# Rotary embeddings: the rotated half made by VectorE across partitions, in place of a matmul with a constant matrix

## The reference

```python
def apply_rope(x, ang):
    d2 = x.shape[-1] // 2
    x1, x2 = xf[..., :d2], xf[..., d2:]
    c, s = cos(ang), sin(ang)
    return concatenate([x1 * c - x2 * s, x2 * c + x1 * s], axis=-1)
# retention: over all 128 features of a head, angles from the token's position
# axial: over the first 64 features with the row of the token, over the last 64 with its column,
#        so the partners lie 32 features apart
```

## Time and profile before

| | us |
|---|---|
| median of 3 runs | 1290.53 (1287.97 to 1294.03) |
| the profiled execution | 1291.3 |
| its span, first to last instruction | 1289.5 |
| TensorE busy | 1266.9 (98%) |
| VectorE busy | 870.5 (68%) |
| ScalarE busy | 718.4 (56%) |
| mean granted TensorE clock | 0.985 of full |

### The profile page before, as it was taken

How to read it: one execution, slowest core, us unless ns; L and a number is a source line. 1 busy time by engine, 2 the same in 40 slices (tenths; PEclk the granted TensorE clock), 3 DMA queues, 4 the chain that set the end, 5 groups by cost and what they waited for, 6 DMA issues and landing times.

```text
span 1289.5 us, 22440 instructions
## 1 busy us (share of the span) xinstructions
PE 1266.9 (98%) x8876; PEld 1171.4 (91%) x8876; DVE 870.5 (68%) x1140; ACT 718.4 (56%) x1070; POOL 49.8 (4%) x76
## 2 busy tenths in 40 slices
PE   8999999999999999999999999999999999999999
PEld 7998899999898779999999899889999988899998
DVE  6889878886889657555566676575555577655554
ACT  3676554444644557444457764665555667655554
POOL 0101000000111000000001000000000000000000
PEclk8899899999899999999999999999999999999999
DMA  9986889995699733555555544356565543466540
GB/s 352 376 305 239 300 269 333 330 332 202 218 346 354 240 83 130 197 197 197 201 187 191 173 148 154 131 179 208 200 195 196 196 146 99 137 206 204 199 163 34
DMA packets 147362, 275.54 MB, mean 214 GB/s; under 512 B 4728, under 2 KB 85392, under 8 KB 147161
## 3 DMA queue, kind: packets, MB, share of 16 engines
q1 hardware_dynamic: 132176, 220.21, 50.1%
q0 software_dynamic: 13872, 52.05, 11.8%
q10 hardware_dynamic: 1240, 2.26, 0.5%
HBM read 273.40 MB, written 1.10 MB: 213 GB/s over the span
## 4 chain that ended last, share of the span: by engine, by line
PE 80%; DVE 10%; DMA 4%; ACT 3%; issue 2%; ACTq 0%; POOL 0%; DVEq 0%; POOLq 0%
PE ps L2006 78%; DMA ada_ring<-in_ada_w 4%; DVE acc_a L1241 3%; DVE wlo L1228 3%; ACT whi L526 1%; PE ps L2147 1%; PE ps L2383 1%; DMA voh<-in_voh 1%; DVE h L1321 0%; ACT xn L583 0%; DVE x L1330 0%; DVE xn L1344 0%; DVE gg L1285 0%; PE ps L2491 0%; DVE acc_a L1238 0%
## 5 line engine op out<-in xcount | busy, mean ns | idle before, releaser
L1228 DVE TENSOR_TENSOR wlo<-raw,whi 128x1024 fp32r<-128x1024 f32 x400 | 484.6, 1225 | 303.3 <-ACT whi L526 302.8
L526 ACT CAST whi<-raw 128x1024 fp32r<-128x1024 f32 x400 | 416.7, 1049 | 421.9 <-PE ps L2006 410.4
L2006 PE MATMUL ps<-hhi,whi 128*128 128x256 f32 x1792 | 499.5, 279 | 4.5 <-DVE wlo L1228 1.9
L2006 PE MATMUL ps<-hhi,wlo 128*128 128x256 f32 x1792 | 492.8, 275 | 0.0
L2006 PE MATMUL ps<-hlo,whi 128*128 128x256 f32 x1792 | 492.8, 275 | 0.0
L2006 PEld LDWEIGHTS ps<-hhi,whi 128*128 128x128 f32 x1792 | 343.8, 192 | 10.6 <-issue 6.4
L2006 PEld LDWEIGHTS ps<-hlo,whi 128*128 128x128 f32 x1792 | 343.8, 192 | 3.9 <-issue 2.4
L2006 PEld LDWEIGHTS ps<-hhi,wlo 128*128 128x128 f32 x1792 | 344.1, 192 | 0.0
L2006 PE MATMUL ps<-whi,hidhi 128*128 128x512 f32 x432 | 164.3, 380 | 0.0
L2006 PE MATMUL ps<-wlo,hidhi 128*128 128x512 f32 x432 | 163.7, 379 | 0.0
L2006 PE MATMUL ps<-whi,hidlo 128*128 128x512 f32 x432 | 163.7, 379 | 0.0
(11 more groups left out here) (238 smaller groups left out, 1168.6 us busy)
## 6 DMA issues: line engine op xcount, KB each, us to landing
raw<-in_ffn_w_in SPq DMA_DIRECT2D x44, 1024.0 KB, 6.3
ada_ring<-in_ada_w POOLq DMA_DIRECT2D x40, 1024.0 KB, 7.3
raw<-in_w_mlp_up SPq DMA_DIRECT2D x32, 1024.0 KB, 5.4
raw<-in_w_mlp_down SPq DMA_DIRECT2D x32, 1024.0 KB, 4.9
raw<-in_ffn_w_out SPq DMA_DIRECT2D x22, 1024.0 KB, 5.0
raw<-in_att_w_qkv SPq DMA_DIRECT2D x18, 1024.0 KB, 6.5
raw<-in_w_in_even SPq DMA_DIRECT2D x18, 1024.0 KB, 4.9
raw<-in_hyb_w_in SPq DMA_DIRECT2D x10, 1024.0 KB, 10.9
```

The source lines that it names most:

```text
L526: A.copy(whi[:, H % 4, :], raw[:, slot(n), h * HALF:(h + 1) * HALF]).then_inc(s["hi_ready"], 1)
L1228: V.tensor_tensor(wlo[:, H % 4, :], raw[:, slot(n), h * HALF:(h + 1) * HALF], whi[:, H % 4, :].bitcast(F32), ALU.subtract).then_inc(s["lo_ ...
L2006: return pe.matmul(out, lhsT, rhs, start=first, stop=last, skip_group_check=True)
```

## The change

The matrix `rotm`, its two DMAs and the nine matmuls with it are gone, and with them the PSUM banks they wrote and the waits for these banks. VectorE makes the rotated half itself: it multiplies rows 64 to 127 of `f` by the sine and writes the product to rows 0 to 63 of `pt3[0]`, and the other way round; then it multiplies `f` by the cosine into `pt3[1]` and adds the two into `f`. That is four instructions for three. The sign that the matrix carried is in the sine table now (plus in rows 0 to 63, minus in 64 to 127). For the axial layer, whose partners lay 32 rows apart, the query and key columns of the weights and the two gain vectors come in another order, so that partners lie 64 rows apart there too; the scores are sums over all rows, so this order doesn't show in them. Because both `pt3` halves are used in each step, a step waits for the one before it (`rp_done`, `ax_roped`).

```diff
@@ GpSimd queue
-            pool.dma_start(rotm[:, :], t["rot_ret"]).then_inc(s["even_in"], 16)
...
-            pool.dma_start(rotm[:, :], t["rot_ax"]).then_inc(s["even_in"], 16)
@@ VectorE
+            def rotate(f):
+
+                r, c = [pt3[:, i, :].rearrange("p (a b) -> p a b", a=2) for i in range(2)]
+                for to, at in ((slice(0, 64), slice(64, P)), (slice(64, P), slice(0, 64))):
+                    V.tensor_tensor(r[to], f[at], bcast(rope[at, 1, :], 2), ALU.mult)
+                link(V.tensor_tensor(c, f, bcast(rope[:, 0, :], 2), ALU.mult))
+                return V.tensor_tensor(f, c, r, ALU.add)
+
             def ret_rope(i):
 
                 f = f3l[:, 512 * i:512 * i + 512].rearrange("p (a b) -> p a b", a=2)
-                r = pt3[:, i % 2, :].rearrange("p (a b) -> p a b", a=2)
-                dve.wait_ge(s["rp_rot"], i + 1)
-                dve.wait_ge(s["sw_o"], 8)
-                V.tensor_tensor(f, f, bcast(rope[:, 0, :], 2), ALU.mult)
-                link(V.tensor_tensor(r, ps[:, i, :].rearrange("p (a b) -> p a b", a=2), bcast(rope[:, 1, :], 2),
-                                     ALU.mult))
-                V.tensor_tensor(f, f, r, ALU.add).then_inc(s["rp_done"], 1)
+                dve.wait_ge(s["proj_free"], 20 + i // 2)
+                if i:
+                    dve.wait_ge(s["rp_done"], i)
+                else:
+                    dve.wait_ge(s["sw_o"], 8)
+                rotate(f).then_inc(s["rp_done"], 1)
...
             def ax_rope(i):
 
                 f = f3l[:, AX_CHUNKS[i]:AX_CHUNKS[i] + 512].rearrange("p (a b) -> p a b", a=2)
-                r = pt3[:, i % 2, :].rearrange("p (a b) -> p a b", a=2)
-                dve.wait_ge(s["ax_rot"], i + 1)
-                V.tensor_tensor(f, f, bcast(rope[:, 0, :], 2), ALU.mult)
-                link(V.tensor_tensor(r, ps[:, AX_ROT_BANK[i], :].rearrange("p (a b) -> p a b", a=2),
-                                     bcast(rope[:, 1, :], 2), ALU.mult))
-                V.tensor_tensor(f, f, r, ALU.add).then_inc(s["ax_roped"], 1)
+                dve.wait_ge(s["ax_done"], i + 1)
+                if i:
+                    dve.wait_ge(s["ax_roped"], i)
+                rotate(f).then_inc(s["ax_roped"], 1)
@@ TensorE
             sw_values(7)
-            ret_rotate(0)
-            ret_rotate(1)
             even_half(7, 0)
-            ret_rotate(2)
-            ret_rotate(3)
             even_half(7, 1)
...
-            ax_rotate(0)
             proj_half("B", 6, HI + 5, 3)
...
             proj_half("B", 4, HI + 7, 1, parts=(0,))
-            ax_rotate(1)
             proj_half("B", 4, HI + 7, 1, parts=(1,))
             proj_half("B", 4, HI + 8, 2, parts=(0,))
-            ax_rotate(2)
             proj_half("B", 4, HI + 8, 2, parts=(1,))
...
             ax_values(1)
-            ax_rotate(3)
             pe.wait_ge(s["ax_ln"], 5)
             ax_out(0)
...
             ax_turn(3)
-            ax_rotate(4)
             ax_out(1)
@@ tables
-    out["rope_ret"] = np.stack([np.cos(a), np.sin(a)], 1)
-    out["rot_ret"] = rotation(64)
+    out["rope_ret"] = np.stack([np.cos(a), np.sin(a) * sign], 1)
```

More of the change, by code:

```diff
@@ L80 @@
 bias_in0 bias_in1 bias_in2 dl_bias0 dl_bias1 dl_s0 dl_s dl_z dl_e dl_t dl_tc dl_td dl_o dl_r dl_y dl_yhi dl_ylo gate_added
-even_in nr_sq nr_ssq nr_ln nr_r nr_done rp_rot rp_done
+even_in nr_sq nr_ssq nr_ln nr_r nr_done rp_done
 dec_step dec_ready rt_sig rt_g rt_s rt_p rt_o rt_sq rt_ssq rt_ln rt_r rt_y rt_hi rt_lo
 sw_s sw_z sw_e sw_pn sw_t sw_tc sw_tl sw_o qkv_hi qkv_lo sw_sink sw_hi sw_lo
-ax_sq ax_ssq ax_ln ax_r ax_done ax_rot ax_roped ax_khi ax_klo ax_s ax_z ax_e ax_pn ax_t ax_tc ax_o ax_hi ax_lo
+ax_sq ax_ssq ax_ln ax_r ax_done ax_roped ax_khi ax_klo ax_s ax_z ax_e ax_pn ax_t ax_tc ax_o ax_hi ax_lo
 out_done dve_step act_step one_ready
@@ L175, in program @@
             rope = sb(r, "rope", [P, 2, S])
-            rotm = sb(r, "rotm", [P, P])
             lgam = sb(r, "lgam", [P, 4, 8])
@@ L215, in program @@
         AX_CHUNKS = [8 * S] + [512 * i for i in range(4)]
-        AX_SSQ_BANK, AX_ROT_BANK = (0, 0, 1, 6, 4), (1, 2, 3, 0, 1)
+        AX_SSQ_BANK = (0, 0, 1, 6, 4)
         def pair_of(b):
@@ L1772, in _ @@
             next_split(0, 1)
-            dve.wait_ge(s["even_in"], 16 * 5)
+            dve.wait_ge(s["even_in"], 16 * 4)
             V.tensor_scalar(nsink[:, :], sinkt[:, :], -1.0, None, ALU.mult)
@@ L1944, in _ @@
             split(H0 + 6)
-            dve.wait_ge(s["even_in"], 16 * 7)
+            dve.wait_ge(s["even_in"], 16 * 5)
             ax_norm(0)
@@ L2504, in sw_values @@
                 m.then_inc(s["sw_o"], 1)
[L2506 to L2515, removed]
             def ret_scores(h):
@@ L2650, in ax_sums @@
                 mm(ps[:, AX_SSQ_BANK[i], :], ones[:, :], sq3[:, i % 2, :]).then_inc(s["ax_ssq"], 1)
[L2652 to L2656, removed]
             def ax_scores(h):
@@ L2664, in ax_scores @@
                     pe.wait_ge(s["ax_e"], 2 * h - 2)
-                if 4 <= h < 6:
-                    pe.wait_ge(s["ax_roped"], h)
                 kh = qkhi[:, 0, (h // 4) * S:(h // 4 + 1) * S]
@@ L2679, in ax_turn @@
                     pe.wait_ge(s["ax_tc"], h)
-                else:
-                    pe.wait_ge(s["ax_roped"], 2)
                 for u in range(2):
@@ L2690, in ax_values @@
                 pe.wait_ge(s["ax_tc"], h + 1)
-                if h == 0:
-                    pe.wait_ge(s["ax_roped"], 3)
-                elif h % 2 == 0:
+                if h and h % 2 == 0:
                     pe.wait_ge(s["ax_lo"], h // 2)
@@ L2725, in _ @@
             proj_half("B", 6, HI + 4, 2)
-            pe.wait_ge(s["even_in"], 16 * 7)
-            ax_rotate(0)
             proj_half("B", 6, HI + 5, 3)
@@ L2731, in _ @@
             ax_sums(1)
-            pe.wait_ge(s["ax_roped"], 1)
             ax_sums(2)
             proj_half("B", 4, HI + 7, 1, parts=(0,))
-            ax_rotate(1)
             proj_half("B", 4, HI + 7, 1, parts=(1,))
             proj_half("B", 4, HI + 8, 2, parts=(0,))
-            ax_rotate(2)
             proj_half("B", 4, HI + 8, 2, parts=(1,))
@@ L2835, in angles @@
         return (pos.astype(f)[:, None] * inv[None, :]).astype(f).T
[L2837 to L2842, removed]
+    sign = np.where(np.arange(P) < 64, f(1), f(-1))[:, None]
     a = np.concatenate([angles(np.arange(S), P)] * 2)
-    out["rope_ret"] = np.stack([np.cos(a), np.sin(a)], 1)
-    out["rot_ret"] = rotation(64)
+    out["rope_ret"] = np.stack([np.cos(a), np.sin(a) * sign], 1)
     ar, ac = angles(np.arange(S) // 64, 64), angles(np.arange(S) % 64, 64)
-    a = np.concatenate([ar, ar, ac, ac])
-    out["rope_ax"] = np.stack([np.cos(a), np.sin(a)], 1)
-    out["rot_ax"] = rotation(32)
+    a = np.concatenate([ar, ac, ar, ac])
+    out["rope_ax"] = np.stack([np.cos(a), np.sin(a) * sign], 1)
     return {k: np.ascontiguousarray(v) for k, v in out.items()}
@@ L2856, in layout, with halves_apart @@
     import numpy as np
+    def halves_apart(a):
+        a = np.asarray(a)
+        return a.reshape(a.shape[:-1] + (-1, 2, 2, 32)).swapaxes(-3, -2).reshape(a.shape)
     def c(a):
@@ L2867, in layout @@
         "ret_norm": c(v["ret_norm_2"]), "swa_q": c(v["swa_q_norm_2"]), "swa_k": c(v["swa_k_norm_2"]),
-        "ax_q": c(v["ax_q_norm_2"]), "ax_k": c(v["ax_k_norm_2"]),
+        "ax_q": c(halves_apart(v["ax_q_norm_2"])), "ax_k": c(halves_apart(v["ax_k_norm_2"])),
     }
@@ L2872, in layout @@
     vtab = np.concatenate([tables, np.ones((1, 32), tables.dtype)], 0)
-    return {"cols": np.ascontiguousarray(cols), "vtab": np.ascontiguousarray(vtab)}
+    w = np.array(v["w_in_odd_2"])
+    w[..., :1280] = halves_apart(w[..., :1280])
+    return {"cols": np.ascontiguousarray(cols), "vtab": np.ascontiguousarray(vtab), "w_in_odd_2": w}
 DIRECT = ["x", "ada_w", "ada_b", "norm_post", "ffn_w_in", "ffn_w_out", "hyb_w_in", "hyb_w_out", "pool_w", "att_w_qkv",
```

## The result

| | before | after |
|---|---|---|
| median, us | 1290.64 (8 runs) | 1298.37 (8 runs, 1297.58 to 1305.51) |
| the profiled execution, its span, us | 1291.3, 1289.5 | 1298.29, 1296.5 |
| mean granted TensorE clock | 0.985 | 0.986 |

A forecast was written before the change was run, and what follows sets the result against it. TensorE, busy 98%, was taken to bound the kernel, but to wait for VectorE's longer steps: 2.75 (retention wait) + 1.9 (clock) + 2.15 (axial) = 6.8 us slower, 1297.3 us from the median 1290.5; range 1292.5 to 1300.5.

The forecast's parts named there:

- the side of no change: Whole kernel: time within 0.5% (6.5 us) of the kernel before; chance 52%.
- The view: Whole kernel: TensorE is busy 98% of the span, so read its timeline beside VectorE's around the nine rotations.
- Length of a product over 64 rows: VectorE's rotary step: a 64-row product costs what a whole one does, near 0.69 us, since length goes by columns.
- The rival of half length: VectorE's rotary step: 64 rows take half the time, a step 2.03 us, total within 1 us of 1290.5; 4%.
- Streamed or waited: VectorE's rotary step: instructions start 0.72 us apart (waited, 2.88 us a step, chosen) or overlap (streamed, 2.53 us).
- The retention wait: Before ret_scores(0): TensorE goes on 2.75 us later than today, after an idle gap of 6.2 us.
- The clock fall: Behind the retention gap: granted clock falls to 0.50, costing 1.9 us, bounds 0 to 4.8 us.
- The axial walk: Axial place, 1043 to 1100 us: longer VectorE steps delay TensorE place by place, ending 2.15 us later.
- No gap exceeds about 2.2 us, like the 1.91 us that left the clock up.: Axial place: TensorE's gaps stay at or below about 2.2 us, so the clock was expected to hold there.
- a rival of 8%: Axial place: the clock falls a second time, another 1.9 us, 8.7 us slower in all, 1299.2 us; 8%.
- The faster rival: Whole kernel: TensorE's queue alone counts, 7.7 us come off, 1282.8 us, if VectorE finishes the retention steps by 785.5; 3%.

The follow-up runs named there:

- e3_row_zero: Changed kernel with every instruction of the rotary step starting at row 0, one 64-row product to scratch and one over all rows; 1301.45 us (single run).
- e1_ret_only: Kernel before with only the retention place changed, the axial place keeping its matmul rotations; 1298.84 us, 1.0067 of the kernel before.
- e8_late_wide: e1_ret_only with two retention steps over 1024 columns instead of four over 512, left behind sw_ylo(3); 1293.76 us (single run).
- e2_axial_only: Kernel before with only the axial place changed, the retention place keeping its four matmul rotations; 1293.53 us, 1.0024 of the kernel before.
- e9_again: The changed kernel run once more, unaltered, for a second profile; 1298.1 us.
- e6_early_wide: e1_ret_only with two retention steps over 1024 columns, begun earlier, before next_split(6, 2) and next_split(7, 0); 1288.38 us, 0.9980 of the kernel before.
- e4_own_rows: Changed kernel with each 64-row product writing to the rows it reads, so nothing crosses; 1297.47 us (single run).

## Why the prediction held

The forecast was 1297.3 us and the measured median 1298.37, within its range; the sign and the mechanism were the ones given. The median is above 1297.0, on the side to which the prediction had given 45%, against 52% for the side of no change. By its own steps:

- **The view.** The page says 98% busy and the profile after shows the trap in it: 9.1 us less work and 7.7 us more time.
- **Length of a product over 64 rows**, taken from ScalarE's copies: 0.69 expected, 0.69 measured. The rival of half length is out.
- **Streamed or waited.** Waited, as chosen: VectorE's chain from the first product to the end of the last sum took 790.39 - 776.69 = 13.70 us, 13.8 expected. Two errors cancel in that. The products start 0.70 apart and a step takes 2.73 us up to what follows it, not 2.88, except the first, after which the next step waits for `rp_done` (779.61 - 776.69 = 2.92). And a split with a step behind it takes 1.25 us (782.34 to 783.59), not 1.14, because that step's first product is held as well. e3_row_zero is the streamed end, and its wait is 16.63 - 15.01 = 1.62 us longer. The prediction says 1.6, though its own 790.4 less 788.92 gives 1.5.
- **The retention wait.** 2.80 us for 2.75, gap 6.06 for 6.2.
- **The clock fall.** Right in kind and mis-sized: 1.9 us had been taken as half of the 3.8 us in which the clock came back at the start of the trace. Here it stayed low behind the gap for 3 us in one execution and over 6 in another, 1.53 and 3.08 us of loss; e1_ret_only 3.05, e8_late_wide 2.72. One row at the start of a trace gave the size only to a factor of 1.6; the bounds of 0 to 4.8 hold all of them. That trace held four more low stretches, of 3.4 to 10.2 us (at 32.6, 145.3, 336.4 and 490.0), which the prediction didn't read and which show how far the length varies. That the sum came near is in part luck: one price for the fall stood for two quite different ones.
- **The axial walk.** In e2_axial_only against the earlier trace rows, less 0.17: the row sums +0.74 (0.86 expected), `ax_scores(0)` +0.72 (0.86), `ax_scores(4)` +1.66 (1.72), `ax_out(2)` +2.07 (2.15); with its fifth rotation gone between, as said. Each is about 0.1 short, which fits the 2.73 us a step. The walk's 1063.47 for the end of `ax_klo(1)` has no row beside it; measured, it was 1063.51 - 0.17 = 1063.34.
- **"No gap exceeds about 2.2 us, like the 1.91 us that left the clock up."** This step failed. The gaps are as expected (1.64 and 1.97), but behind the second the granted clock was 0.50 in the first profile (1.58 us lost) and 1.00 in e9_again. One gap of 1.91 us that cost nothing was no proof that 1.97 us never would; the second fall, held for a rival of 8%, happened in two of the five executions with gaps of 1.85 to 1.97 us there. It can be the larger part of why the median is 1.1 above the forecast, but a profile shows one execution and the median many, so that is argued and not shown.
- **The faster rival** had the right point of decision: VectorE must be done by the time TensorE arrives. e6_early_wide is that case, made by moving the steps and not by making them shorter.

The sum by the measured terms is 2.80 + 1.53 + 3.65 = 7.98 us in one execution and 2.81 + 3.08 + 2.07 = 7.96 in the other, for 6.8 expected and 7.73 between the medians. That two such different splits give the same sum is chance.

## What to carry to other kernels

Work taken off the busiest engine pays only where what it waits for next is early by at least as much; look, place by place, at when the other engine would have to begin. Here a VectorE product over half the rows cost what one over all rows cost (0.69 us at 512 columns), and changing the starting row added about 0.1, so splitting by rows doubled the cost. Where a new gap before matmuls can't be avoided, count the low clock behind it as a second price (1.5 to 3.1 us behind the gaps of 3.4 to 6.1 us here), and if the other engine has idle time ahead, start the step there.

## What the runs showed of the hardware that was not expected

- The hold between VectorE's neighbours follows the starting row of input and output, not whether rows are crossed: 0.60 us from start to start at the same row, about 0.70 to 0.72 at another, in a kernel where nothing crosses (e4_own_rows).
- Behind the same gap of 6.1 us in the same program TensorE worked at the low clock for about 3 us once and over 6 us once, always at 0.50, the lower of the two levels (1.2 GHz); it was busy all that while. A longer gap didn't cost more: a gap of 3.42 us in e8_late_wide cost 2.72.
- A gap of 1.97 us, with one of 1.64 us some 9 us ahead of it, brought the clock down in one of two profiled executions of the same kernel.
- The clock also fell with no gap at all, at the end of 32 records of one-column matmuls (at 490.0 in the kernel before, 3.4 us long).
